# Sums of squares by rounded squares and remainders in the heads stage, with three steps moved on ScalarE and VectorE

## The reference

```
qkv = silu(causal_short_conv(concat[gq, gk, gv], conv_w))
q_g = l2norm(cq) * GDN_DK ** -0.5          # l2norm(x) = x * rsqrt(sum(x * x) + EPS)
k_g = l2norm(ck)
...
T = triangular_solve(eye + A)              # A from k k^T, beta and the decays
u = T @ (v * beta);  w = T @ (k * beta * exp(gam))
... chunked recurrence over S, rmsnorm, gate, branch projection
```

## Time and profile before

| | |
|---|---|
| median of 3 runs | 1378.74 us (1378.68 to 1378.74) |
| profiled execution | 1378.71 us |
| its span, first to last instruction | 1377.0 us |
| TensorE busy | 1361.5 us (99%) |
| VectorE busy | 1025.3 us (74%) |
| ScalarE busy | 802.5 us (58%) |
| mean granted TensorE clock | 0.999 of full speed |

### The profile page before, as it was taken

How to read it: one execution, slowest core, us unless ns; L and a number is a source line. 1 busy time by engine, 2 the same in 40 slices (tenths; PEclk the granted TensorE clock), 3 DMA queues, 4 the chain that set the end, 5 groups by cost and what they waited for, 6 DMA issues and landing times.

```text
span 1377.0 us, 25249 instructions
## 1 busy us (share of the span) xinstructions
PE 1361.5 (99%) x9088; PEld 1237.0 (90%) x9088; DVE 1025.3 (74%) x1603; ACT 802.5 (58%) x1311; POOL 23.5 (2%) x71
## 2 busy tenths in 40 slices
PE   8999999999999999999999999999999999999998
PEld 8999999988888888888899999999999898888887
DVE  5786786677666687666788888888888877666665
ACT  4444554654433454444577898898898854544443
POOL 6000000000000000000000000000000000000000
PEclk9999999999999999999999999999999999999999
DMA  8574555555555646666574454453553286566661
GB/s 266 151 192 140 150 142 170 186 184 192 198 191 184 216 129 207 197 197 184 153 185 131 130 134 117 130 159 98 149 133 122 73 209 209 162 207 195 198 186 61
DMA packets 298383, 227.82 MB, mean 165 GB/s; under 512 B 10882, under 2 KB 280404, under 8 KB 298324
## 3 DMA queue, kind: packets, MB, share of 16 engines
q1 hardware_dynamic: 298324, 227.01, 55.6%
HBM read 225.90 MB, written 1.08 MB: 165 GB/s over the span
## 4 chain that ended last, share of the span: by engine, by line
PE 96%; DVE 2%; ACT 1%; DVEq 0%; DMA 0%; issue 0%; ACTq 0%
PE G L1984 9%; PE G L1986 8%; PE G L1985 8%; PE M L1989 7%; PE M L2001 7%; PE M L1990 7%; PE G L2001 7%; PE M L1991 7%; PE G L2003 4%; PE M L2003 4%; PE G L2811 2%; PE G L1989 2%; PE G L1991 2%; PE G L1990 2%; PE G L2104 2%; PE M L2617 1%
## 5 line engine op out<-in xcount | busy, mean ns | idle before, releaser
L1161 DVE TENSOR_TENSOR w_lo<-w_raw,w_hi 128x2048 fp32r<-128x2048 f32 (+2 forms) x249 | 481.1, 1936 | 154.3 <-ACT w_hi L627 150.2
L627 ACT ACTIVATE w_hi<-w_raw 128x2048 fp32r<-128x2048 f32 x198 | 377.7, 1908 | 170.4 <-PE G L1986 73.1
L1984 PE MATMUL G<-xa,w_hi 128*128 128x256 f32 x960 | 282.7, 295 | 0.0
L1986 PE MATMUL G<-xa,w_lo 128*128 128x256 f32 x960 | 271.3, 283 | 0.0
L1985 PE MATMUL G<-xa,w_hi 128*128 128x256 f32 x960 | 271.1, 282 | 0.0
L1984 PEld LDWEIGHTS G<-xa,w_hi 128*128 128x128 f32 x960 | 183.3, 191 | 1.8 <-DVE w_lo L1161 0.7
L1985 PEld LDWEIGHTS G<-xa,w_hi 128*128 128x128 f32 x960 | 183.4, 191 | 0.0
L1986 PEld LDWEIGHTS G<-xa,w_lo 128*128 128x128 f32 x960 | 183.0, 191 | 0.0
L1989 PE MATMUL M<-w_hi,xb 128*128 128x512 f32 x304 | 119.0, 391 | 0.6 <-DVE xb L1161 0.5
L1990 PE MATMUL M<-w_lo,xb 128*128 128x512 f32 x304 | 118.7, 390 | 0.0
L1991 PE MATMUL M<-w_hi,xb 128*128 128x512 f32 x304 | 118.3, 389 | 0.0
(11 more groups left out here) (424 smaller groups left out, 2546.1 us busy)
## 6 DMA issues: line engine op xcount, KB each, us to landing
w_raw<-in_w_in SPq DMA_DIRECT2D x150, 512.0 KB, 4.9
w_raw<-in_ffn_w_in SPq DMA_DIRECT2D x88, 512.0 KB, 5.0
w_raw<-in_w_ff SPq DMA_DIRECT2D x64, 512.0 KB, 4.3
w_raw<-in_ffn_w_out SPq DMA_DIRECT2D x44, 512.0 KB, 4.7
w_raw<-in_w_in SPq DMA_DIRECT2D x33, 256.0 KB, 3.2
w_raw<-in_w_out SPq DMA_DIRECT2D x16, 512.0 KB, 4.1
w_raw<-in_w_branch_gdn SPq DMA_DIRECT2D x16, 512.0 KB, 5.3
w_raw<-in_w_branch SPq DMA_DIRECT2D x12, 512.0 KB, 4.3
```

The costliest lines, as they stand in the source:

```text
L627: nc.scalar.activation(w_hi[:, slot, :], w_raw[:, slot, :], ACT.Copy).then_inc(hi_ready, 1)
L1161: return v.tensor_tensor(dst, src, hi.bitcast(F32), ALU.subtract)
L1984: mm(out_, w[0], x[0], start=first, stop=False)
L1986: return mm(out_, w[1], x[0], start=False, stop=last_)
```

## The change

- The squares of query and key are rounded to fp32r by VectorE into `sq_hi`, and the remainders written to `sq_lo`. TensorE multiplies each by fp32r ones (`ones_r`) and adds both in the same bank: the first before the value transposes, where the 32-bit product was, the second after `quarter(15)` (head 0: behind the transposes).
- ScalarE copies the values (line 1088) behind `split_j(2)` and ahead of the logarithm, no longer behind `token_rstd`.
- VectorE's second half of the low part of chunk 3 moves from the end of a pass to the start of the next, ahead of `decayed(1)`; in the last pass (chunk `FIRST["yh"]`) it stands behind `scored(1)`. The first half of chunk 5 moves from ahead of `inverse(2)` to behind `middle(5)`.
- A semaphore `lo_first` lets TensorE begin `quarter(0)` with the first half alone; `quarter(1)` waits for the whole. `early_yh` is changed alike.
- `hgrn_gate` comes ahead of the clamp of `eh`. Some semaphores are merged.

```diff
+    sq_hi, sq_lo = (part[:, 13:15, :].rearrange("p k t -> p (k t)") for part in (xb_hi, xb_lo))
@@ ScalarE, head
             split_j(2)
             if gemm:
+                act.wait_ge(vt_done, i + 1)
+                nc.scalar.activation(vsd, M[:, 0, :].rearrange("p (i e c) -> p i e c", i=TT, e=2), ACT.Copy).then_inc(v_ready, 1)
                 act.wait_ge(ss_done, i + 1)
...
-            if gemm:
-                act.wait_ge(vt_done, i + 1)
-                nc.scalar.activation(vsd, M[:, 0, :].rearrange("p (i e c) -> p i e c", i=TT, e=2), ACT.Copy).then_inc(v_ready, 1)
             split_j(3)
@@ VectorE, head
+            if main and gemm:
+                w_low_half(c0 + 3 + RING - 6, 1, i, 6)
             decayed(1)
...
-            if main and gemm:
-                w_low_half(c0 + 5 + RING - 6, 0, i, 6)
+            if not gemm:
+                w_low_half(FIRST["yh"], 1)
             inverse(2)
...
             middle(5)
+            if main and gemm:
+                w_low_half(c0 + 5 + RING - 6, 0, i, 6)
             decayed(4)
...
             if gemm:
+                dve.wait_ge(sq_ready, i + 1)
+                v.tensor_copy(sq_hi, eg[:, 0:2 * T]).then_inc(sqh_ready, 1)
                 w_low_half(c0 + 1 + RING, 1, i, 6)
+                settle()
+                low_of(sq_lo, eg[:, 0:2 * T], sq_hi).then_inc(sql_ready, 1)
...
-                w_low_half(c0 + 3 + RING, 0, i, 6)
+                w_low_half(c0 + 3 + RING, 0, i, 6).then_inc(lo_first, 1)
                 dve.wait_ge(lt_ready, i + 1)
                 diag = lt.rearrange("p e (b c) -> p e b c", b=3)[:, :, 0:3:2, :]
                 v.tensor_tensor(diag, diag, tri[:].unsqueeze(1).unsqueeze(1).to_broadcast([P, 2, 2, P]), ALU.mult)
-                w_low_half(c0 + 3 + RING, 1, i, 6)
@@ TensorE, head
                     if part == 1:
-                        weights_ready(c0 + i * 6)
+                        if main:
+                            pe.wait_ge(lo_first, i)
+                        else:
+                            weights_ready(c0)
...
+                if j == 0 and n == 1:
+                    weights_ready(c0 + i * 6)
...
-                pe.wait_ge(sq_ready, i + 1)
-                mm(M[:, 2, :], ones[:], eg[:, 0:2 * T], start=True, stop=True).then_inc(ss_done, 1)
+                pe.wait_ge(sqh_ready, i + 1)
+                mm(M[:, 2, :], ones_r, sq_hi, start=True, stop=False)
...
             if main:
                 quarter(15)
+            if gemm:
+                pe.wait_ge(sql_ready, i + 1)
+                mm(M[:, 2, :], ones_r, sq_lo, start=False, stop=True).then_inc(ss_done, 1)
```

More of the change, by code:

```diff
@@ L296, in emit @@
     dots_done, relu_ready, relu_used = sem("dots_done"), sem("relu_ready"), sem("relu_used")
-    forget_step, fln_ready, cum_done = (sem(n) for n in ("forget_step", "fln_ready", "cum_done"))
+    forget_step, fln_ready, forget_done = (sem(n) for n in ("forget_step", "fln_ready", "forget_done"))
     va_ready = sem("va_ready")
-    wi_done, decay_step, ab_done = sem("wi_done"), sem("decay_step"), sem("ab_done")
+    decay_step, decay_done = sem("decay_step"), sem("decay_done")
     c_turned_step, ck_loaded, mck_ready = sem("c_turned_step"), sem("ck_loaded"), sem("mck_ready")
@@ L321, in emit @@
     vecs_loaded, vec_done, vec_ready = (sem(n) for n in ("vecs_loaded", "vec_done", "vec_ready"))
-    abln_ready, gsum_done, lb_exp = (sem(n) for n in ("abln_ready", "gsum_done", "lb_exp"))
+    abln_ready, lb_exp = (sem(n) for n in ("abln_ready", "lb_exp"))
+    lo_first = sem("lo_first")
     hpv_done, hsq_ready, hss_done, hrs_ready, hfin, lt2_ready, qk_ready = (
@@ L337, in emit @@
                          "ntc_ready"))
+    sqh_ready, sql_ready = sem("sqh_ready"), sem("sql_ready")
     vn0_done, vn0_ready, cross_done, r1_ready, vn1_done, vn1_ready, go_done = (
@@ L341, in emit @@
         sem(n) for n in ("gsq_ready", "gss_done", "grs_ready", "ogh_ready", "ogl_ready"))
-    gate_tanh, gate2_tanh = sem("gate_tanh"), sem("gate2_tanh")
+    gate_tanh = sem("gate_tanh")
     ohh_ready, ohl_ready, ym_ready, ymh_ready, yml_ready = (
@@ L1050, in head @@
                 own = gates2[:, ds(i - 1, 1), :, :].rearrange("p n b t -> p (n b t)")
-                nc.scalar.activation(own, own, ACT.Tanh, scale=0.5).then_inc(gate2_tanh, 1)
+                nc.scalar.activation(own, own, ACT.Tanh, scale=0.5).then_inc(gate_tanh, 1)
                 act.wait_ge(wl_ready, i * 8)
@@ L1176, in w_low_half @@
                 ins.then_inc(lo_ready, 1)
+            return ins
         def x_low_half(n, h):
@@ L1212, in _ @@
         qi_copy(0)
-        dve.wait_ge(wi_done, 1)
+        dve.wait_ge(forget_done, 1)
         v.tensor_copy(wi, M[:, 4, 0:TT * SMALL].rearrange("p (i h) -> p i h", i=TT))
@@ L1248, in _ @@
         add_scores(0)
-        dve.wait_ge(cum_done, 1)
+        dve.wait_ge(forget_done, 2)
         v.tensor_copy(c_f, M[:, 5, 0:TT * NH].rearrange("p (i h) -> p i h", i=TT)).then_inc(c_turned_step, 1)
         qi_copy(2)
-        dve.wait_ge(cum_done, 2)
+        dve.wait_ge(forget_done, 3)
         v.tensor_copy(c_turned[0:TT * NH, :], M[0:TT * NH, 5, P:2 * P]).then_inc(c_turned_step, 1)
@@ L1627, in _ @@
         w_low(FIRST["ba"] + RING)
-        dve.wait_ge(ab_done, 1)
+        dve.wait_ge(decay_done, 1)
         v.tensor_copy(abx, M[:, 5, 0:4 * VH].rearrange("p (i h) -> p i h", i=TT))
@@ L1828, in head @@
             if not main:
-                dve.wait_ge(gsum_done, 1)
+                dve.wait_ge(decay_done, 2)
                 sums = M[:, 4, 0:3 * VH].rearrange("p (i h e) -> p i h e", i=3, e=2)
@@ L1862, in head @@
                     w_low_half(FIRST["yh"] + 2, 1)
+            if main and gemm:
+                hgrn_gate(i)
             if gemm:
@@ L1865, in head @@
                 v.tensor_scalar(eh, eh, 2.0 ** 62, None, ALU.min).then_inc(eh_ready, 1)
-            if main and gemm:
-                hgrn_gate(i)
-            if gemm:
                 v.tensor_copy(yi, ident[:].unsqueeze(1).unsqueeze(1).to_broadcast([P, TT, 2, P]))
@@ L1938, in sum_low @@
             low_of(xa_lo[:, 2 * u:2 * u + 2, :], o_h[:, 2 * u:2 * u + 2, :], xa_hi[:, 2 * u:2 * u + 2, :]).then_inc(yml_ready, 1)
-        dve.wait_ge(gate2_tanh, GH)
+        dve.wait_ge(gate_tanh, 6 + GH)
         for n in range(4):
@@ L2190, in _ @@
                                       ident[0:SMALL, 0:SMALL])
-        ins.then_inc(wi_done, 1)
+        ins.then_inc(forget_done, 1)
         static_chunk(2, col_gemm)
@@ L2198, in _ @@
         mm(M[:, 5, NH:2 * NH], ones[:], log_f[:, 0, :], start=True, stop=False)
-        mm(M[:, 5, NH:2 * NH], tri[:], log_f[:, 1, :], start=False, stop=True).then_inc(cum_done, 1)
+        mm(M[:, 5, NH:2 * NH], tri[:], log_f[:, 1, :], start=False, stop=True).then_inc(forget_done, 1)
         static_chunk(3, col_gemm)
@@ L2202, in _ @@
         pe.wait_ge(c_turned_step, 1)
[L2203 removed]
+        nc.tensor.transpose(M[0:TT * NH, 5, P:2 * P], c_f.rearrange("p i h -> p (i h)"), ident[:]).then_inc(forget_done, 1)
         static_chunk(4, col_gemm)
@@ L2407, in ab_turned @@
                                           ident[0:2 * VH, 0:2 * VH])
-            ins.then_inc(ab_done, 1)
+            ins.then_inc(decay_done, 1)
         def sums_of_g():
@@ L2413, in sums_of_g @@
                 mm(M[:, 4, VH * b:VH * b + VH], tri[:], gdec[:, b, :], start=True, stop=True)
-            mm(M[:, 4, 2 * VH:3 * VH], ones[:], gdec[:, 0, :], start=True, stop=True).then_inc(gsum_done, 1)
+            mm(M[:, 4, 2 * VH:3 * VH], ones[:], gdec[:, 0, :], start=True, stop=True).then_inc(decay_done, 1)
         c0 = FIRST["heads"]
@@ L2467, in early_yh @@
             if n == 0:
-                weights_ready(c)
+                pe.wait_ge(lo_first, GH)
                 pe.wait_ge(evac[0], EV_Y[0])
@@ L2495, in early_yh @@
                 yh_w_hi(3, (3,))
+                weights_ready(c)
                 pe.wait_ge(ohh_ready, 3)
```

## The result

The changed kernel takes 1381.33 us (19 runs, 1381.02 to 1381.85) where the kernel before takes 1378.74 us (19 runs, 1378.44 to 1379.37). The ratio is 1.0018, with a 95% interval of 1.0012 to 1.0024: 2.6 us more, a difference that the interval tells from none, but smaller than 0.2%. The forecast was 1380.7 us.

A forecast was written before the change was run, and what follows sets the result against it. Two bounds equal to within some 0.1 us: TensorE, and a second loop TensorE-ScalarE-VectorE-TensorE. Terms 2.4 (six passes) - 0.2 - 0.33 + 0.15 = +2.0 us on 1378.71 gave 1380.7 us; range 1374.9 to 1382.0 us.

The forecast's parts named there:

- the rival of the whole copy: Rival: the copy costs its whole 0.58 us on the second loop, nothing absorbed; 1381.8 us; chance 0.2.
- Two loops, and the longer one counts: Per pass, the second loop grows by 0.41 us, TensorE's own falls by 0.48; the pass takes 50.56 us.
- the second loop: TensorE to ScalarE's token_rstd to VectorE's delta_gate and inverse(1) to TensorE's inv_z(2); about as long as TensorE's 50.16 us.
- TensorE's gain: 0.38 us in each of 8 heads from the fp32r ones products, plus 0.10 us in 7 passes at quarter 18.
- the wait at quarter 18: TensorE's second product there waits for the copy of the values; the earlier copy saves 0.10 us in 7 passes.
- The loop's growth: The copy delays token_rstd by 0.48 us, 0.07 absorbed at delta_gate; 0.40 us a pass, six times: +2.4 us.
- nothing gained, nothing lost: Half (3, 1), moved from pass end to ahead of decayed(1): 1.14 us out and 1.14 in on the second loop.
- Three signs of the prediction: Waits at line 2759 would mean late squares; TensorE busy some 3 us less; ones product 0.24 us twice.
- First pass: Head 0: the 1.14 us put before inverse(1) leaves half of TensorE's 0.38 us gain: -0.2 us.
- Pass 7: After the last inv_z(2) wait: 0.48 us gain less 0.15 waiting for lt_pre at line 2759: -0.33 us.
- Last pass: Half 1 of yh's low part, 1.14 us, put into a 0.95 us wait ahead of inverse(2): +0.15 us.
- Nothing: Rival: VectorE makes up part of the delay, the second loop grows 0 to 0.2 us; 1378.4 to 1379.6 us; chance 0.1.

The follow-up runs named there:

- The double copy: Changed kernel with ScalarE's copy of the values made twice in a row, a drain between: 1385.65 us, ratio 1.0050.
- the one without the squares: Changed kernel with inverse(1) ahead of half (4, 0), lt_pre ahead of delta_gate, and the 32-bit product of ones and squares restored: 1377.68 us.
- both edits: Changed kernel with inverse(1) ahead of the first half low part of chunk 4, and lt_pre ahead of delta_gate: 1374.50 us, ratio 0.9973.
- the copy alone: Kernel before with only ScalarE's copy of the values moved behind the third conversion: 1381.62 us, ratio 1.0022.
- the pair with the copy back: Changed kernel with ScalarE's copy back behind token_rstd, 1382.76 us; the same with half (3, 1) also back ahead of nt, 1378.10 us.
- the same edit: inverse(1) put ahead of the first half low part of chunk 4: 1376.55 us on the changed kernel, 1384.00 us on the kernel before.

## Why the prediction was right, and where its sizes were off

**What the total can show.** The range of the prediction, 1374.9 to 1382.0 us, takes in the values of all its rivals, so that the time alone confirms little; 1381.33 us is 0.6 from the forecast and 0.5 from the rival of the whole copy. What decides is the pass, its waits and the experiments.

**Two loops, and the longer one counts: right.** With the second loop shortened, the same TensorE work takes 49.58 us a pass, with it as changed 50.51. The double copy shows that the loop binds microsecond for microsecond. The Trainium skill's rule, "Perfetto Trace Analysis", section "Identifying the Most-Contended Engine", to optimize the engine with the highest occupancy first, would have given 1375.0 us. The trace disagrees for this change: TensorE's matmul share was 99%, its weight loads' share, which that section prefers as a measure for TensorE, 90%, both the highest, and TensorE's work fell, but the time rose. It agrees once the second loop is short (1374.5 us).

**TensorE's gain: right.** 0.39 us a head for the squares, against 0.38. The rest of the change gives TensorE 50.15 - 49.97 = 0.18 us a pass where the second loop is short (the pass before against the one without the squares), against 0.10 forecast for the wait at quarter 18. The rest lies right behind that wait. TensorE with both edits and without the squares:

```profile
917.74 0.39 PE L1994 MATMUL M<-w_hi,xa 128*128 128x512 f32 x1
917.97 0.39 PE L1995 MATMUL M<-w_lo,xa 128*128 128x512 f32 x1
...
920.46 0.59 PE L2770 MATMUL M<-arena 128*128 128x256 f32 x2
```

The first product of quarter 18 takes a step of 0.23 us, against 0.34 before, and from the second one to the key and query products it is 920.46 - 917.97 = 2.49, against 921.32 - 918.76 = 2.56: 0.11 and 0.07. Why the products behind the wait were slower isn't shown. The squares' work on VectorE, 0.43 and 0.69 us, lies within the bounds and is hidden, as foreseen: `w_low_j(2)` starts 0.03 us behind its conversion in both kernels.

**The loop's growth: right in kind, a little large.** 0.35 us a pass was measured, 0.40 forecast: 2.1 us and not 2.4 in six steps. Its working was right at `delta_gate` (a wait of 0.49, start 0.03 after the release). From `delta_gate` to `inverse(1)`, with the same half low parts between, it is 932.54 - 917.99 = 14.55 us before and 934.01 - 919.50 = 14.51 after: 0.04 of the 0.05 lie there.

**What was missed: the paths over `lt_pre` and `nt`.** The prediction costed `lt_pre` only in pass 7, and called the half's move "nothing gained, nothing lost". It named `inv_z(2)` as the place where TensorE gets its operand just in time, and `inv_z(1)` was one too (the copy alone, above). TensorE waits for `lt_pre` in every pass (0.4 us). That wait only takes from the later one at `inv_z(2)`, 0.65 us where 0.8 to 0.9 were forecast; the loop sets the pass either way, so that the sum of the pass didn't suffer. Three signs of the prediction failed with it. A wait at the products of line 2759 was to mean that the squares are late, and it came though they are not: the remainders are there at 912.70 + 0.69 = 913.39, 1.15 us ahead of their product. TensorE's busy time was to fall by some 3 us, and the page has 0.6 less. And the ones products take 0.32 and 0.23 us, not 0.24 twice. That the move isn't neutral is shown by the pair with the copy back: 1382.76 with the half at its new place, 1378.10 with it at its old one. Half (5, 0) hides in its new place, as forecast: it ends ahead of `decayed(4)`, which still waits 0.17 us for ScalarE.

**The ends, each a mis-sized term.** Four terms were given for them.
- First pass: -0.2 forecast, +0.04 measured. In head 0 there is no `delta_gate`, but the copy delays the exponential too. VectorE's timeline there, changed kernel:

```profile
716.89 0.70 DVE L1883 TENSOR_TENSOR arena<-arena 128x512 f32<-128x512 f32 x1 [1.43 <-ACT arena L1077]
```

Before, this operation started at 716.30, so it is 0.59 us later; `lt_pre` follows it. TensorE's key and query products wait for it here too, so that `nt` starts only 0.11 us earlier than before (722.54, 722.65), where TensorE had been 0.33 ahead at the value transposes (714.35, 714.68). `inverse(1)` comes at 731.97, where the forecast had about 731.7.
- Pass 7: -0.33 forecast, +0.03 measured. The delay falls from 2.16 us to 1.52 ahead of the key and query products (1073.08 against 1071.56). There the wait for `lt_pre`, as large as in the other passes, brings it to 1.77 (1073.99 against 1072.22), 0.25 where 0.15 was forecast. Then the prediction has no term for what follows: at the start of the last pass the weight load waits 0.51 us for ScalarE's line 961, and the delay is 2.16 again (1082.57 against 1080.41). The wait of 0.21 us for `inverse(1)` behind it was in the kernel before too.

```profile
1082.57 0.19 PEld L2451 LDWEIGHTS G<-xa,w_hi 128*128 128x128 f32 x1 [0.51 <-ACT xa L961]
```
- Last pass: +0.15 forecast, +0.6 measured. The half (1.14 us) was to hide in a wait of 0.95 ahead of `inverse(2)`. But VectorE reaches that place later: the half starts 1087.39 - 1085.26 = 2.13 us after the load of `inv_z(2)`, where the wait before began 1085.68 - 0.95 - 1083.07 = 1.66 after it. 1.14 - 0.95 + 0.47 = 0.66, and `inv_z(3)` is late by 0.64 against `inv_z(2)`. Of the 0.47 us, 0.37 lie between the starts of `scored(0)` and `middle(3)` (1085.64 and 1086.51, before 1083.45 and 1083.95). The rows, changed kernel:

```profile
1085.64 0.41 DVE L1732 TENSOR_TENSOR arena<-M,ident 128x256 f32<-128x256 f32 x1
1086.51 0.43 DVE L1708 TENSOR_TENSOR arena<-arena 128x256 f32<-128x256 f32 x1 [0.46 <-issue]
...
1087.39 1.23 DVE L1163 TENSOR_TENSOR w_lo<-w_raw,w_hi 128x1024 fp32r<-128x1024 f32 x1
```
```profile
1089.30 0.52 PEld L2632 LDWEIGHTS M<-arena 128*128 128x128 f32 x4 [0.84 <-DVE arena L1752]
```

The measured terms, 0.04 + 2.1 + 0.03 + 0.6, make the 2.8 us of the span. Against the forecast's 2.0 the pass term gave back 0.3 and the three ends took 0.24 + 0.36 + 0.45 = 1.05: +0.75, which is the 0.6 us by which the forecast is low, to within the spread of the runs.

**The rivals.** The whole copy at 0.58 a pass (1381.8 us) is excluded by the pass, 50.51 us and not 50.74, though its total lies only 0.5 us off. "Nothing" is excluded by the pass as well, and by the interval; that interval, some 1.7 us wide, also shows that the prediction took the measurement to be coarser than it is when it said that 2.8 us can hardly be told from none.

**Left open.** What holds VectorE ahead of `middle(3)` in the last pass: the profile shows no releaser for that gap of 0.46 us.

## What to carry to other kernels

An engine that is busy 99% of the time may still not be what sets the pass. Follow each operand that comes just in time back over the other engines; where the way leads round the loop with a slack of hundredths of a microsecond, anything put on it is paid in every pass, though the engines on it are idle for several microseconds. A filler that is moved takes its cover with it: price it by the waits at the place that it leaves, too, since the same edit gained 4.8 us in one order and lost 5.4 us in the other. To see whether a loop binds, double one thing on it, and look whether the pass grows by exactly that.

## What the runs showed of the hardware

Two products of 512 columns in fp32r replace one in 32 bit. TensorE's timeline, changed kernel:

```profile
911.99 0.61 PE L2732 MATMUL M<-arena 128*128 128x128 f32 x4
912.35 0.48 PE L2740 MATMUL M<-xb 128*128 128x512 f32 x1
912.67 0.60 PE L2743 MATMUL M<-ident,arena 128*128 128x128 f32 x4
...
914.54 0.39 PE L2750 MATMUL M<-xb 128*128 128x512 f32 x1
914.77 0.38 PE L2718 MATMUL M<-ident,arena 128*128 128x128 f32 x2
```

And the four 32-bit products ahead, in the kernel before:

```profile
910.90 0.61 PE L2717 MATMUL M<-arena 128*128 128x128 f32 x4
```

The second takes a step of 914.77 - 914.54 = 0.23 us; the first, set between 32-bit products, 912.67 - 912.35 = 0.32. Over the whole pass the gain is nonetheless 0.39 us, since the 0.09 us are given back just ahead: the four 32-bit products take 912.35 - 911.99 = 0.36 us in front of the fp32r product, and 911.35 - 910.90 = 0.45 in front of the 32-bit one. In sum 0.86 + 0.45 - 0.32 - 0.23 - 0.36 = 0.40. VectorE rounds 512 elements a partition in 0.43 us, and takes 0.69 for the remainder, which has a second operand.
